# Value products of two heads side by side in the column halves of the array, gathered by six in two attentions

## The chip, the cores and the metric

The kernel runs on one core of one Trainium2 chip. The metric is the device time of one execution in microseconds (us). Engines: TensorE (PE: matmuls; PEld: its weight loads), VectorE (DVE), ScalarE (ACT), GpSimd (POOL) and SyncE (SP), which issues the DMAs.

## The reference, cut to what matters

The program is three transformer layers one after another over 512 tokens, width 1024. There are four attentions, and only they are touched here:

```python
# first layer, 16 meta keys beside the 512:
attn = softmax(s1) - lam * softmax(s2); y_a = attn @ v     # "diff": 4 heads, values 128 wide
y_b = softmax(s_window, sink) @ v                           # "win": 8 heads, values 64 wide
# second layer: dense causal, 8 heads, keys 96 wide, values 64 wide ("mla")
y_mla = softmax(causal(q @ k.T)) @ v
# third layer ("nsa"), 16 heads, values 64 wide, three gated branches per head:
y = g0 * (p_cmp @ vc) + g1 * (p_slc @ vs) + g2 * (p_win @ vw)
```

With 512 tokens the selected blocks and the 512 window both come to plain causal attention, so "nsa" has two causal branches (b = 0, 1) and one over 31 compressed keys. Everything else is projections and MLPs, each product made from three f16 matmuls (lines 845 to 847).

## The kernel before, in words

**Slots, tiles, units, chunks.** An attention is a run of slots. A slot is one head (and in "nsa" one branch of one head). Two heads (half 0 and half 1) make one output tile of 128 rows, 64 rows a head: half 0 gives rows 0 to 63, half 1 rows 64 to 127. "diff" is different: its two slots are the two softmaxes of one head whose values are 128 wide. So a tile is 2 slots, in "nsa" 4. Runs: "mix" is 8 slots of diff, then 8 of win; "mla" has 8 slots; "nsa" has 32 (8 tiles).

Each slot is worked twice. First the natural pass: queries on partitions, three or four *chunks* (`nat_scores`, line 947, with a mask product at 953 or 955) in two PSUM banks in turn; VectorE takes the row maximum (`nat_max`, line 1738), ScalarE the exponentials with their sums (`nat_exp`, line 1256). From these come a log-sum per row, which is split into f16 pieces (`split_lse`), turned by TensorE (`turn_lse`, line 1019) and written as extra rows of the queries (`lse_to_rows`, line 1804). Then the key pass: keys on partitions, three or four *units* (`key_scores`, lines 978 and 986) in three PSUM banks; ScalarE writes exp, already normalised, to one of four f32 tiles `tmp` (`key_exp`, line 1273), and TensorE multiplies with the values into the PSUM bank of the tile (`unit_values`, line 1006; an *extra* unit with all small keys of a tile at line 1003, its scores at 972). The causal units of a slot have one product of 512 columns, one of 384 and one of 128, and one of 256. The f32 value products are two instructions each. The 64 value columns of a head stand beside 64 columns of zeros (`vzm`, `vz`, zeroed by two memsets), so that each product writes all 128 rows and adds nothing to the other head's.

**Order.** The order is written out by hand and the same on all engines. The natural pass runs `ahead` slots before the key pass (4 in mix and nsa, 3 in mla). So a run begins with `ahead` slots of chunks alone (the prologue), then has slots with chunks and units, and its last `ahead` slots have units alone. Within a slot TensorE goes by steps:

```python
key_scores(t, i); [turn_lse]; nat_scores(nxt, i); unit_values(t.u + i - 2)
```

ScalarE per step does the exponential of this step's unit, then the one of the last step's chunk. The waits that pace this are: a unit's scores wait for the exponential three units back, a chunk's for the one two chunks back, an exponential of a unit for the value product four units back (its tile in `tmp`), a value product for its exponential.

Of the kernel before, what the change touches and what calls it, by code (L numbers as in the profile page):

```python
# [19 lines left out]

# [14 lines left out]
P = 128  # L35
# [181 lines left out]
class Slot:  # L217
# [3 lines left out]
    def __init__(self, kind, j, half, b, c, u, lse, y):  # L221
# [6 lines left out]
        self.c, self.u, self.lse, self.y = c, u, lse, y  # L228
        self.n_units = len(self.keys) + self.extra


class Run:
# [3 lines left out]
    def __init__(self, kinds, ahead, c, u, lse, y):  # L236
        self.slots, self.pre, self.ahead = [], [], ahead
        self.branches = kinds[0].branches
# [5 lines left out]
        for k in kinds:  # L244
            for j in range(k.tiles):
                for half in range(2):
                    for b in range(k.branches):
                        s = Slot(k, j, half, b, c, u, lse, y)
                        self.slots.append(s)
# [23 lines left out]
    def joined(self, s):  # L273
        t = self.at(s + 3)
# [23 lines left out]
UNITS = {s.u + i: (s, i) for s in ALL_SLOTS for i in range(s.n_units)}  # L298
# [153 lines left out]
def build_program(nc, x_in, stream, consts, params, aux, out):  # L452
    ctx = ExitStack()
    with ctx:
# [72 lines left out]
        def pair(at, shape):  # L527
# [34 lines left out]
            "p (a b c) -> p a b c", a=NQ, b=4)  # L562
        cqs, at = pair(at, [6, T])
# [29 lines left out]
        def values(t, kb):  # L593
# [3 lines left out]
            a = t.half * HD  # L597
            if t.kind.name == "win":
                return vw[:, kb, a:a + P]
            if t.kind.name == "mla":  # L600
                return vzm[:, kb, t.j, a:a + P]
            at = t.j // 4 * 3 * HD + a
            return vz[:, kb, t.b, at:at + P]

        def extra_values(t):
# [3 lines left out]
            return vmw if t.kind.name == "win" else vcz[:, 2 * (t.j // 4) + t.j % 2, :]  # L609

# [200 lines left out]
        def _(pe):  # L811
# [146 lines left out]
            def key_scores(t, i):  # L958

                u = t.u + i  # L960
# [28 lines left out]
            def unit_values(u):  # L989

                t, i = UNITS[u]
                new = t.first and i == 0
                end = t.last and i == t.n_units - 1
                if new and t.y >= 2:
# [4 lines left out]
                pe.wait_ge(key_exped, u + 1)  # L999
                p = tmp[:, u % 4, :]  # L1000
                o = y_bank(t.y)
                if i == len(t.keys):
                    mm = pe.matmul(o, extra_values(t), p, start=False, stop=end)  # L1003
                else:
                    for n_, (kb, c0, q0, n) in enumerate(t.keys[i]):
                        mm = pe.matmul(o[:, q0:q0 + n], values(t, kb), p[:, c0:c0 + n], start=new and n_ == 0,  # L1006
                                       stop=end and n_ == len(t.keys[i]) - 1)
                mm.then_inc(unit_av, 1)

            def turn_lse(t):  # L1010

                pe.wait_ge(lse_split, t.lse + 1)
                if t.kind.name in ("diff", "win"):
                    e = (t.tile + (8 if t.kind.name == "win" else 0)) // 2 - 1
# [12 lines left out]
            def attention(run):  # L1027

                for kind, n, c in run.pre:
                    extra_scores(kind, n, c)  # L1030
                for s in range(-run.ahead, run.n):
                    t, nxt = run.at(s), run.at(s + run.ahead)
                    if t is not None and (t.b == 0):
                        pe.wait_ge(lse_rows, t.lse + 1)
                    e = run.ended(s - 2)
                    if e is not None and e.kind.name == "diff":
                        sum_squares(e.j)
                    for i in range(run.steps(s)):
                        if t is not None and i < t.n_units:
                            key_scores(t, i)  # L1040
# [4 lines left out]
                        if t is not None and i < t.n_units and t.u + i >= run.u0 + 2:  # L1045
# [1334 lines left out]
```

## Time and profile before

| | |
|---|---|
| median of 3 runs | 2185.51 us (2184.99 to 2186.41) |
| the profiled execution, its own time | 2186.2 us |
| its span | 2184.4 us |
| TensorE busy | 2071.3 us (95%) |
| VectorE, ScalarE busy | 1195.7 us (55%), 817.0 us (37%) |
| mean granted TensorE clock | 0.964 of full |

The span is the time from the first to the last instruction in the trace; the execution's own time lies 1.8 us around it. A record of a matmul holds its latency too: in a stream the distance between starts, not the record's length, is what one costs. The clock is given as a share of 2.4 GHz.

### The profile page before, as it was taken

The numbers are of one execution on the slowest core, as the hardware profiler recorded it, in microseconds if no ns is written. First come the engines' busy times: TensorE is split into PE (matmuls) and PEld (weight loads), VectorE is DVE, ScalarE is ACT, GpSimd is POOL, SyncE is SP. The second block draws the span as 40 slices with busy tenths as digits, with TensorE's granted clock in tenths as the row PEclk, the third lists the DMA queues.
The fourth block names the chain that finished last, engine by engine and source line by source line (L and its number), as shares of the span: only waits on it lengthen the run. The fifth ranks groups of instructions, "written<-read, shape, count | busy, mean of one in ns | idle before, by whom it ended". The sixth has DMA issues, their size and how long they took to land. (4 is left out here: it accounts for less than half of the span.)

```text
span 2184.4 us, 27324 instructions
## 1 busy us (share of the span) xinstructions
PE 2071.3 (95%) x10625; PEld 1008.3 (46%) x10625; DVE 1195.7 (55%) x2186; ACT 817.0 (37%) x1481; POOL 38.5 (2%) x40
## 2 busy tenths in 40 slices
PE   7989999999999989989899999899799998999996
PEld 3444544444444434445344444355456653444442
DVE  5956744546554348665576522367555545855222
ACT  3437732323232222445343222234167742422220
POOL 2000000000000002000000000000000000000000
PEclk9979999999999999999899999898889998999998
DMA  6300133324333313212143333235000021433311
GB/s 196 107 1 1 59 87 106 97 77 126 106 97 116 97 49 116 87 39 87 39 132 100 107 105 97 77 109 174 11 1 1 20 87 29 145 101 102 109 46 39
DMA packets 52184, 179.18 MB, mean 82 GB/s; under 512 B 5984, under 2 KB 9696, under 8 KB 51680
## 3 DMA queue, kind: packets, MB, share of 16 engines
q1 hardware_dynamic: 52064, 177.51, 27.2%
q8 instruction: 84, 1.38, 0.3%
q14 instruction: 36, 0.29, 0.0%
HBM read 174.34 MB, written 2.10 MB: 81 GB/s over the span
## 5 line engine op out<-in xcount | busy, mean ns | idle before, releaser
L1540 DVE SCALAR_TENSOR_TENSOR w_lo<-w_raw,w_hi 128x1024 f16<-128x1024 f32 x317 | 385.4, 1219 | 181.4 <-ACT w_hi L1202 161.1
L1202 ACT ACTIVATE w_hi<-w_raw 128x1024 f16<-128x1024 f32 x317 | 331.0, 1049 | 277.4 <-PE pS L847 271.3
L845 PE MATMUL pS<-arena,w_hi 128*128 128x512 f16 x924 | 350.2, 379 | 5.0 <-DVE w_lo L1540 3.1
L845 PE MATMUL pS<-xx,w_hi 128*128 128x512 f16 x928 | 352.6, 380 | 1.4 <-DVE xx L1555 1.4
L846 PE MATMUL pS<-xx,w_hi 128*128 128x512 f16 x928 | 352.5, 380 | 0.0
L847 PE MATMUL pS<-xx,w_lo 128*128 128x512 f16 x928 | 352.4, 380 | 0.0
L846 PE MATMUL pS<-arena,w_hi 128*128 128x512 f16 x924 | 350.2, 379 | 0.0
L847 PE MATMUL pS<-arena,w_lo 128*128 128x512 f16 x924 | 350.2, 379 | 0.0
L1211 ACT ACTIVATE arena<-src 128x512 f16<-128x512 f32 x106 | 66.7, 629 | 325.1 <-DVE src L2113 168.2
L1595 DVE TENSOR_TENSOR tmp<-pS,rs 128x512 f32<-128x512 f32 x98 | 67.5, 689 | 140.2 <-PE pS L847 140.2
L1006 PE MATMUL pO<-tmp,arena 128*128 128x512 f32 (+3 forms) x384 | 144.1, 475 | 0.0
L845 PEld LDWEIGHTS pS<-arena,w_hi 128*128 128x128 f16 x924 | 90.5, 98 | 115.4 <-DVE w_lo L1540 3.6
L847 PEld LDWEIGHTS pS<-xx,w_lo 128*128 128x128 f16 x928 | 90.9, 98 | 110.2 <-issue 1.1
L847 PEld LDWEIGHTS pS<-arena,w_lo 128*128 128x128 f16 x924 | 90.4, 98 | 109.1
L846 PEld LDWEIGHTS pS<-arena,w_hi 128*128 128x128 f16 x924 | 90.4, 98 | 108.7 <-issue 0.3
L845 PEld LDWEIGHTS pS<-xx,w_hi 128*128 128x128 f16 x928 | 91.0, 98 | 107.4 <-DVE xx L1555 2.2
L846 PEld LDWEIGHTS pS<-xx,w_hi 128*128 128x128 f16 x928 | 90.9, 98 | 105.4 <-issue 1.5
L1273 ACT ACTIVATE tmp<-pS 128x256 f32<-128x256 f32 (+2 forms) x184 | 99.4, 541 | 71.8 <-PE pS L986 40.6
L889 PE MATMUL pS<-xx,w_hi 128*128 128x512 f16 x192 | 77.8, 405 | 30.0 <-DVE xx L1555 15.8
L978 PE MATMUL pS<-arena 128*128 128x512 f16 (+3 forms) x480 | 103.9, 314 | 1.3 <-DVE arena L1804 1.3
L2091 DVE TENSOR_SCALAR xx<-pS 128x512 f32<-128x512 f32 x24 | 16.6, 692 | 144.3 <-PE pS L847 144.3
L1738 DVE TENSOR_REDUCE st_max<-pS 128x1 f32<-128x512 f32 (+2 forms) x112 | 55.9, 517 | 64.4 <-PE pS L955 46.6
(319 smaller groups left out, 2822.2 us busy)
## 6 DMA issues: line engine op xcount, KB each, us to landing
w_raw<-in_w SPq DMA_DIRECT2D x317, 512.0 KB, 3.6
X<-in_x SPq DMA_DIRECT2D x1, 2112.0 KB, 8.2
arena<-in_c SPq DMA_DIRECT2D x2, 1024.0 KB, 5.5
out_t<-X SPq DMA_DIRECT2D x8, 256.0 KB, 2.0
arena<-in_h SPq DMA_DIRECT2D x4, 256.0 KB, 14.7
arena<-in_h SPq DMA_DIRECT2D x2, 512.0 KB, 9.1
arena<-in_c SPq DMA_DIRECT2D x2, 256.0 KB, 2.8
arena<-arena SPq DMA_DIRECT2D x4, 128.0 KB, 2.5
```

The source lines that it names most:

```text
L845: pe.matmul(ps, wh, ah, start=f, stop=False)
L846: pe.matmul(ps, wh, al, start=False, stop=False)
L847: mm = pe.matmul(ps, wl, ah, start=False, stop=l)
L889: pe.matmul(ps, wh, xa[0][:, k, 0:T], start=k == 0, stop=False)
L978: pe.matmul(ps[:, c0:c0 + n], k[:, ks_], q[:, qs], start=x == 0, stop=False)
L1006: mm = pe.matmul(o[:, q0:q0 + n], values(t, kb), p[:, c0:c0 + n], start=new and n_ == 0, stop=end and n_ == len(t.keys[i]) - 1)
L1202: act.activation(w_hi[:, u % WR, :], w_raw[:, u % RAW, :], ACT.Copy, scale=WS).then_inc(hi_split, 1)
L1211: act.activation(dst, a, ACT.Identity, scale=scale).then_inc(rhs_hi, 1)
L1273: act.activation(tmp[:, u % 4, 0:a.shape[1]], a, ACT.Exp).then_inc(key_exped, 1)
L1540: dve.scalar_tensor_tensor(out=w_lo[:, u % WR, :], in0=w_raw[:, u % RAW, :], scalar=WS, in1=w_hi[:, u % WR, :], op0=ALU.mult, op1=ALU.subt ...
L1595: dve.tensor_tensor(dst, ps, r[:, 0:T], ALU.mult).then_inc(evicted, 1)
L1738: ins = dve.tensor_reduce(stat(st_max, t)[:, x:x + 1], nat_bank(c)[:, c0:c0 + n], AX.X, ALU.max, negate=True)
```

## The change

For win, mla and nsa (`paired`), the zeros beside the values go: a value product has 64 stationary columns and writes only the 64 rows of its own head, `o[rows, ...]`. The units of the two heads of a tile alternate (`number`), so that products for the lower and the upper column half follow one another. In win two units are multiplied together; in mla and nsa six, that is, all units of two heads and one branch. The six wait for the last of their exponentials and are issued when its unit lies two or more units back. For this the exponentials get eight tiles in mla and nsa: the four of `tmp` and four more in space that is free then (`p_mla`, `cbias`). The extra unit stays one product of 128 columns. Both heads' log-sums must be there before a tile's first unit, so the natural pass runs further ahead: 5 slots in mix, 4 in mla, 6 in nsa; the log-sum steps move one slot (nsa: two) earlier with it. `turn_lse` and `sum_squares`, which share a PSUM bank, get a wait for the copy out of it. Two memsets of VectorE go. The diff slots keep their products.

```diff
-        self.c, self.u, self.lse, self.y = c, u, lse, y
+        self.c, self.lse, self.y = c, lse, y
         self.n_units = len(self.keys) + self.extra
+        self.paired = kind.name != "diff"
+        self.u, self.u_end = [], u
...
+        self.values, self.todo = [], defaultdict(list)
...
-                        u += s.n_units
                     lse += 1
+                u = self.number(self.slots[-2 * k.branches:], u)
...
+    def number(self, group, u):
+
+        if group[0].paired:
+            b = len(group) // 2
+            order = [(group[x + h * b], i) for x in range(b) for i in range(len(group[0].keys)) for h in range(2)]
+            order += [(group[-1], len(group[0].keys))] * group[-1].extra
+            n = 2 if group[0].kind.name == "win" else 6
+            self.values += [list(range(u + x, u + x + n)) for x in range(0, 6 * b, n)]
+            self.values += [[u + 6 * b]] * group[-1].extra
+        else:
+            order = [(t, i) for t in group for i in range(t.n_units)]
+            self.values += [[u + x] for x in range(len(order))]
+        for n, (t, i) in enumerate(order):
+            t.u.append(u + n)
+            self.todo[min(n * len(group) // (len(order) - group[0].paired * group[-1].extra), len(group) - 1) + group[0].s].append((t, i))
+        for t in group:
+            t.u_end = u + len(order)
+        return u + len(order)
...
-        return self.at(s + 2 + (not odd)) if s % 2 == odd else None
+        return self.at(s + 4 + (not odd)) if s % 2 == odd else None
 
     def summed(self, s):
-        return self.head(s, 2, 0)
+        return self.head(s, 3, 0)
 
     def turned(self, s):
-        return self.head(s, 1, 1)
+        return self.head(s, 2, 1)
 
     def joined(self, s):
-        t = self.at(s + 3)
+        t = self.at(s + 4)
...
-        return max(a.n_units if a else 0, len(b.nat) if b else 0, 3)
+        return max(len(self.todo[s]) if a else 0, len(b.nat) if b else 0, 3)
+
+    def unit(self, s, i):
+
+        return self.todo[s][i] if 0 <= s < self.n and i < len(self.todo[s]) else None
...
-    for name, kinds, ahead in (("mix", ("diff", "win"), 4), ("mla", ("mla",), 3), ("nsa", ("nsa",), 4)):
+    for name, kinds, ahead in (("mix", ("diff", "win"), 5), ("mla", ("mla",), 4), ("nsa", ("nsa",), 6)):
...
+        p_mla, _ = view(at, [4, T])
...
-            a = t.half * HD
+            a = 2 * t.half * HD
             if t.kind.name == "win":
-                return vw[:, kb, a:a + P]
+                return vw[:, kb, a:a + HD]
             if t.kind.name == "mla":
-                return vzm[:, kb, t.j, a:a + P]
+                return vzm[:, kb, t.j, a:a + HD]
             at = t.j // 4 * 3 * HD + a
-            return vz[:, kb, t.b, at:at + P]
+            return vz[:, kb, t.b, at:at + HD]
...
+        def p_more(t):
+
+            return {"mla": [p_mla[:, n, :] for n in range(4)], "nsa": [cbias[:, n, :] for n in range(4)]}.get(t.kind.name, [])
+
+        def p_tile(t, u):
+
+            more = p_more(t)
+            n = (u - RUNS[t.kind.name].u0) % 8 if more else u % 4
+            return tmp[:, n, :] if n < 4 else more[n - 4]
...
-            def unit_values(u):
-
-                t, i = UNITS[u]
-                new = t.first and i == 0
-                end = t.last and i == t.n_units - 1
-                if new and t.y >= 2:
+            def unit_values(us):
+
+                t, i = UNITS[us[0]]
+                if t.first and i == 0 and t.y >= 2:
                     if t.y < 6:
                         pe.wait_ge(y_scaled, t.y - 1)
                     else:
                         pe.wait_ge(rhs_ready, Y_RHS[t.y - 2] + 1)
-                pe.wait_ge(key_exped, u + 1)
-                p = tmp[:, u % 4, :]
+                pe.wait_ge(key_exped, us[-1] + 1)
                 o = y_bank(t.y)
                 if i == len(t.keys):
-                    mm = pe.matmul(o, extra_values(t), p, start=False, stop=end)
-                else:
+                    pe.matmul(o, extra_values(t), p_tile(t, us[0]), start=False, stop=True,
+                              skip_group_check=t.paired).then_inc(unit_av, 1)
+                    return
+                for x in range(0, len(us), 2):
+                    i = UNITS[us[x]][1]
                     for n_, (kb, c0, q0, n) in enumerate(t.keys[i]):
-                        mm = pe.matmul(o[:, q0:q0 + n], values(t, kb), p[:, c0:c0 + n], start=new and n_ == 0,
-                                       stop=end and n_ == len(t.keys[i]) - 1)
-                mm.then_inc(unit_av, 1)
+                        for u in us[x:x + 2]:
+                            t = UNITS[u][0]
+                            rows = head_rows(t.half) if t.paired else slice(0, P)
+                            new = t.b == 0 and i == 0 and n_ == 0 and (t.paired or t.first)
+                            mm = pe.matmul(o[rows, q0:q0 + n], values(t, kb), p_tile(t, u)[:, c0:c0 + n], start=new, stop=False,
+                                           skip_group_check=t.paired)
+                            if n_ == len(t.keys[i]) - 1:
+                                mm.then_inc(unit_av, 1)
 
             def turn_lse(t):
 
                 pe.wait_ge(lse_split, t.lse + 1)
+                if t.lse:
+                    pe.wait_ge(lse_rows, t.lse)
...
+                left = list(run.values)
                 for s in range(-run.ahead, run.n):
                     t, nxt = run.at(s), run.at(s + run.ahead)
-                    if t is not None and (t.b == 0):
+                    if t is not None and t.first:
+                        pe.wait_ge(lse_rows, t.lse + 1 + t.paired)
+                    elif t is not None and not t.paired:
                         pe.wait_ge(lse_rows, t.lse + 1)
                     e = run.ended(s - 2)
                     if e is not None and e.kind.name == "diff":
+                        if run.turned(s - 1):
+                            pe.wait_ge(lse_rows, run.turned(s - 1).lse + 1)
                         sum_squares(e.j)
                     for i in range(run.steps(s)):
-                        if t is not None and i < t.n_units:
-                            key_scores(t, i)
+                        now = run.unit(s, i)
+                        if now:
+                            key_scores(*now)
                         if i == 1 and run.turned(s):
                             turn_lse(run.turned(s))
                         if nxt is not None and i < len(nxt.nat):
                             nat_scores(nxt, i)
-                        if t is not None and i < t.n_units and t.u + i >= run.u0 + 2:
-                            unit_values(t.u + i - 2)
-                unit_values(run.u1 - 2)
-                unit_values(run.u1 - 1)
+                        while now and left[0][-1] <= now[0].u[now[1]] - 2:
+                            unit_values(left.pop(0))
+                for us in left:
+                    unit_values(us)
...
-                if u >= 4:
-                    act.wait_ge(unit_av, u - 3)
-                act.activation(tmp[:, u % 4, 0:a.shape[1]], a, ACT.Exp).then_inc(key_exped, 1)
+                n = len(p_more(t)) + 4
+                if u >= RUNS["mix" if t.kind.name in ("diff", "win") else t.kind.name].u0 + n:
+                    act.wait_ge(unit_av, u - n + 1)
+                act.activation(p_tile(t, u)[:, 0:a.shape[1]], a, ACT.Exp).then_inc(key_exped, 1)
...
-            link(dve.memset(vzm[:, :, :, HD:2 * HD], 0.0))
...
-            link(dve.memset(vz, 0.0))
```

## Rows read from the trace of the kernel before

**Rows 1.** Page, busy time by engine over the span

```profile
PE 2071.3 (95%) x10625; PEld 1008.3 (46%) x10625; DVE 1195.7 (55%) x2186; ACT 817.0 (37%) x1481; POOL 38.5 (2%) x40
```

**Rows 2.** Stretches: span, length, PE, PEld, DVE, ACT, POOL busy, clock, DMA share, GB/s

```profile
1618.40:1640.60 22.20, 22.15 (x144) 13.85 (x143) 12.52 (x40) 16.10 (x50) 0.00 (x0) 1.00 0.00 1
1455.00:1475.00 20.00, 20.00 (x215) 15.76 (x214) 17.42 (x29) 7.82 (x11) 0.00 (x0) 0.79 0.89 248
```

**Rows 3.** Chain that ended last, nsa: start, us, the three value products of a slot

```profile
1601.28 0.91 PE pO L1006 x2
...
1603.17 0.92 PE pO L1006 x4
...
1605.41 0.49 PE pO L1006 x2
```

**Rows 4.** Timeline, nsa: start us, us; scores of four extra units, once per tile

```profile
1617.53 1.03 PE L972 MATMUL pS<-arena 128*128 128x512 f16 x4
1639.69 1.03 PE L972 MATMUL pS<-arena 128*128 128x512 f16 x4
1751.59 1.03 PE L972 MATMUL pS<-arena 128*128 128x512 f16 x4
1768.09 1.03 PE L972 MATMUL pS<-arena 128*128 128x512 f16 x4
```

**Rows 5.** Timeline, mla: first units of two successive slots, with chunks and without

```profile
975.05 0.81 PE L978 MATMUL pS<-arena 128*128 128x512 f16 x3
981.31 0.81 PE L978 MATMUL pS<-arena 128*128 128x512 f16 x3
1000.07 0.81 PE L978 MATMUL pS<-arena 128*128 128x512 f16 x3
1004.47 0.81 PE L978 MATMUL pS<-arena 128*128 128x512 f16 x3
```

**Rows 6.** Timeline, win: first unit of three successive tiles

```profile
242.03 0.38 PE L978 MATMUL pS<-arena 128*128 128x256 f16 x2
256.26 0.38 PE L978 MATMUL pS<-arena 128*128 128x256 f16 x2
266.12 0.38 PE L978 MATMUL pS<-arena 128*128 128x256 f16 x2
```

**Rows 7.** Timeline: matmuls of 128 and of 16 output rows in turn

```profile
85.58 0.38 PE L846 MATMUL pS<-xx,w_hi 128*128 128x512 f16 x1
85.80 0.38 PE L847 MATMUL pS<-xx,w_lo 128*128 128x512 f16 x1
86.11 0.38 PE L863 MATMUL pT<-w_hi,xx 128*16 128x512 f16 x1
```

**Rows 8.** Timeline: eight f32 weight loads in a row with matmuls of one column

```profile
37.73 0.97 PEld L905 LDWEIGHTS pO<-ones,acc 128*128 128x128 f32 x8
```

**Rows 9.** Timeline, ScalarE in nsa: a unit and the chunk right behind it

```profile
1599.51 0.60 ACT L1273 ACTIVATE tmp<-pS 128x512 f32<-128x512 f32 x1 [0.48 <-PE pS L986]
1600.01 0.66 ACT L1256 ACTIVATE pS<-pS,st_max 128x512 f32<-128x512 f32 x1
```

**Rows 10.** Waits of ScalarE in nsa, 1589 to 1772: us, times, longest

```profile
ACT tmp L1273 <- PE pS L986: 32.1, 65, 0.9
ACT tmp L1273 <- DVE src L1767: 12.7, 8, 2.1
```

**Rows 11.** Timeline, prologues: slot's first chunk, nsa (ScalarE) and mix (TensorE)

```profile
1585.23 0.66 ACT L1256 ACTIVATE pT<-pT,st_max 128x512 f32<-128x512 f32 x1 [1.04 <-DVE st_max L1738]
1589.34 0.66 ACT L1256 ACTIVATE pS<-pS,st_max 128x512 f32<-128x512 f32 x1 [1.01 <-DVE st_max L1738]
...
145.41 0.75 PE L947 MATMUL pS<-arena 128*128 128x512 f16 x2 [0.66 <-ACT pS L1256]
...
150.61 0.61 PE L947 MATMUL pS<-arena 128*128 128x512 f16 x1 [0.38 <-ACT pS L1256]
```

**Rows 12.** Groups by line: the larger memset

```profile
L2130 DVE MEMSET arena<- 128x3072 f32 x1 | 2.6, 2618 | 0.6 <-issue 0.6
```

More of the change, by code:

```diff
@@ L21 @@
+from collections import defaultdict
 from contextlib import ExitStack
@@ L248, in __init__ @@
                         s = Slot(k, j, half, b, c, u, lse, y)
+                        s.s = len(self.slots)
                         self.slots.append(s)
                         c += len(k.nat)
-                        u += s.n_units
                     lse += 1
+                u = self.number(self.slots[-2 * k.branches:], u)
                 y += 1
@@ L297 @@
 CHUNKS = {s.c + i: (s, i) for s in ALL_SLOTS for i in range(len(s.nat))}
-UNITS = {s.u + i: (s, i) for s in ALL_SLOTS for i in range(s.n_units)}
+UNITS = {s.u[i]: (s, i) for s in ALL_SLOTS for i in range(s.n_units)}
 Y_RHS = {s.y: PL.r[s.kind.rhs] + s.j for s in ALL_SLOTS}
@@ L958, in key_scores @@
             def key_scores(t, i):
-                u = t.u + i
+                u = t.u[i]
                 if u == RUNS["mla"].u0:
@@ L998, in unit_values @@
                         pe.wait_ge(rhs_ready, Y_RHS[t.y - 2] + 1)
-                pe.wait_ge(key_exped, u + 1)
-                p = tmp[:, u % 4, :]
+                pe.wait_ge(key_exped, us[-1] + 1)
                 o = y_bank(t.y)
                 if i == len(t.keys):
-                    mm = pe.matmul(o, extra_values(t), p, start=False, stop=end)
-                else:
-                    for n_, (kb, c0, q0, n) in enumerate(t.keys[i]):
-                        mm = pe.matmul(o[:, q0:q0 + n], values(t, kb), p[:, c0:c0 + n], start=new and n_ == 0,
-                                       stop=end and n_ == len(t.keys[i]) - 1)
-                mm.then_inc(unit_av, 1)
+                    pe.matmul(o, extra_values(t), p_tile(t, us[0]), start=False, stop=True,
[3 more added lines that the diff above has]
+                    i = UNITS[us[x]][1]
+                    for n_, (kb, c0, q0, n) in enumerate(t.keys[i]):
+                        for u in us[x:x + 2]:
[6 more added lines that the diff above has]
+                                mm.then_inc(unit_av, 1)
             def turn_lse(t):
                 pe.wait_ge(lse_split, t.lse + 1)
+                if t.lse:
+                    pe.wait_ge(lse_rows, t.lse)
                 if t.kind.name in ("diff", "win"):
-                    e = (t.tile + (8 if t.kind.name == "win" else 0)) // 2 - 1
+                    e = (t.tile - 1 + (8 if t.kind.name == "win" else 0)) // 2 - 1
                     if e > 0:
@@ L1259, in key_exp @@
             def key_exp(t, i):
-                u = t.u + i
+                u = t.u[i]
                 if t.kind.name == "nsa" and i == len(t.keys):
@@ L1333, in attention @@
                     for i in range(run.steps(s)):
-                        if t is not None and i < t.n_units:
-                            key_exp(t, i)
+                        if run.unit(s, i):
+                            key_exp(*run.unit(s, i))
                         if pending is not None:
@@ L1761, in cmp_bias @@
             def cmp_bias(t):
[L1763 removed]
+                u = t.u[len(t.keys)]
                 dve.wait_ge(key_scored, u + 1)
@@ L1857, in attention @@
                             nat_max(nxt, i)
-                        if t is not None and t.kind.name == "nsa" and t.extra and i == len(t.keys):
-                            cmp_bias(t)
+                        now = run.unit(s, i)
+                        if now and now[0].kind.name == "nsa" and now[1] == len(now[0].keys):
+                            cmp_bias(now[0])
                         if i == 0 and run.joined(s):
```

5 lines of the change are left out of this document (2 added, 3 removed).

## The prediction

> **What bounds the kernel now.** I began with the page's busy times: TensorE is busy for 2071.3 of 2184.4 us [rows 1]. The chain of waits says the same inside nsa, the longest attention: it runs through value products, which take 0.91, 0.92 and 0.49 us for the three units of a slot [rows 3], 2.32 us a slot. Then the stretches: of one nsa tile of four slots (22.20 us) TensorE works 22.15, ScalarE 16.10, VectorE 12.52 [rows 2]. So nsa is bound by TensorE, and ScalarE has only about a quarter of the time free. Last the timeline, for the lengths of a tile: 22.16 us while chunks of the natural pass run beside it, 16.50 in the last slots, which have none [rows 4]. In mla a slot is 6.26 with chunks, 4.40 without [rows 5]; in win a tile is 14.23 with, 9.86 without [rows 6].
>
> From these, nsa's key pass is 7 tiles with chunks and 1 without, 7 x 22.16 + 16.50 = 171.6 us; mla's is 5 x 6.26 + 3 x 4.40 = 44.5. A chunk costs TensorE (22.16 - 16.50) / 12 = 0.47 us, a unit's scores (16.50 - 4 x 2.32 - 0.91 - 0.9 for the extra unit's two parts, - 0.4 for two turns) / 12 = about 0.4.
>
> **Step 1, the products.** A group of six holds 2 x 2.32 = 4.64 us of products, in 16 instructions. If an instruction for the lower column half streams while its neighbour for the upper half does, the group takes half, 2.32. The two instructions of one product use the same half, so only the second of one runs beside the first of the next; at the edges one 512 and one 256 instruction stand alone, (0.46 + 0.24) / 2 = 0.35. And the array changes between 128 and 64 columns twice a group. The nearest row is the change to 16 output rows: starts 0.31 apart instead of 0.22 [rows 7], so 0.09 a change, 0.18 a group. Together 2.85: **1.8 us less a group**, if the streams overlap. No row shows an overlap. Its bounds are 2.32 (all of it and no edges) and 4.64 + 0.18 (none). I take the overlap: the instructions are adjacent and share neither output rows nor columns. The Trainium skill measured it on narrow f16 tiles (TensorE: Matmul & The Clock Gate, section "Measured speedup vs the span model"): three column tiles ran 2.38 times as fast as one after another. No run here shows that yet, and no number of mine uses it.
>
> Weight loads must be hidden too. Eight f32 loads of 128 columns in a row took 0.97 us [rows 8], 0.12 each; those of 64 columns lie between half of that and that. Two per instruction pair of 0.46 us fit, even at 0.21.
>
> **Step 2, what ScalarE makes of the groups (nsa with chunks).** TensorE alone would need 22.16 - 2 x 1.8 = 18.6 a tile. But during a group it feeds ScalarE nothing. ScalarE's need is 16.10 of busy time less the tail of a record that the next instruction would overlap (0.60 recorded, 0.50 to the next start [rows 9]), about 73 / 8 = 9 times a tile [rows 10]: 15.2. How much can it have in hand when a group starts? The chunk issued just before waited for the chunk two back, so there is one unit's exponential (0.50) and one chunk (0.66). The next chunk stands in its queue behind the next unit's exponential, whose scores are behind the group on TensorE. So it stands still for 0.47 (last chunk) + 2.85 + 0.4 (next scores) - 1.16 = 2.6 us a group. Twice that, and part of the wait for the extra unit's bias on VectorE, up to 12.7 / 8 = 1.6 now [rows 10], of which I keep 0.6: 15.2 + 5.2 + 0.6 = **21.0 us a tile**, bounds 20.0 and 22.0. Eight tiles of exponentials do not help here: what is missing is scores, three banks of them. So only 1.2 of the 3.6 us reach the end.
>
> **Step 3, running further ahead.** A prologue slot is chunks alone, a round trip TensorE, VectorE, ScalarE: 4.11 us in nsa, 5.20 in mix [rows 11]; for mla, the same chunks as nsa, I take 4.1. nsa gets two more, mla and mix one. What they did before beside units is then gone there: two nsa slots, one mla, one win.
>
> **The sum.**
> nsa: 6.5 tiles x 21.0 + 1.5 x (16.50 - 3.6) + 2 x 4.11 = 136.5 + 19.4 + 8.2 = 164.1, against 171.6: -7.5.
> mla: TensorE's three passes leave ScalarE more room. A group with chunks is 12.52 - 1.8 = 10.7 against ScalarE's (15.2 - 1.1) / 2 + 2.6 = 9.7, so TensorE rules. 2 x 10.7 + 2 x (8.80 - 1.8) + 4.1 = 39.5, against 44.5: -5.0.
> mix: +5.2 for the prologue; one win slot without chunks, -(14.23 - 9.86) / 2 = -2.2; win's products, some 4.4 us a tile, become 2.2 + 0.9 of edges (three pairs) + 6 x 0.09 = 3.6, -0.8 x 4, of which I count -2.0 because two tiles run beside chunks. +1.0.
> Memsets: 2.6 us [rows 12] and a smaller one a third as large on VectorE; TensorE is busy all of the 20.00 us around the larger [rows 2], so 0; 3.5 us if that cover were gone. The new waits in `turn_lse` and `sum_squares` are for a copy a slot old: 0; were it late, all of TensorE stands behind it, some 0.5 us (one copy) in each of 32 places. No DMA or queue changes.
> Sum -11.5. From the profiled execution, 2186.2, that is 2174.7; the median of the runs lies 0.7 lower: **2174 us**. With step 2's bounds, 2167 to 2181.
>
> **The rivals.**
> *ScalarE keeps up.* If it has more in hand at a group's start (chunks ahead of the unit in its queue), a tile is TensorE's 18.6: 6.5 x 2.4 = 15.6 less, 2158. For it: 6.1 us free a tile [rows 2]. Against: the queue order above.
> *No overlap: slower.* If f32 products in two column halves run one after the other, a group is 4.64 + 0.18, and ScalarE stands still 2.6 + 2.0 = 4.6 each. A tile is 15.2 + 9.2 + 0.6 = 25.0, nsa 6.5 x 25.0 + 1.5 x 16.9 + 8.2 = 196, +24.5; mla 2 x 12.7 + 2 x 9.0 + 4.1 = 47.5, +3.0; mix 5.2 - 2.2 + 24 x 0.09 = +5.2. 2218. It decides once a group exceeds about 3.6 us: each 0.1 costs some 2 us. For it: every one of the present narrow matmuls (16 rows) still takes a full stream [rows 7], though all of those are in one column position. This is also the case where the change does not do what it says.
> *Overlap, but the weight loads show.* 16 loads a group at 0.06 to 0.12 are 1.0 to 1.9 us, in 20 groups and four win tiles: +24 to +46 on 2174, held below the last rival; 2200. Against: now the loads run under the streams. The skill (same page, "What overlaps and what doesn't") says a load overlaps running matmuls only when its row group differs; all loads here use all rows. By that rule this rival would be the case. The trace does not agree for full-width products: a tile has 13.85 us of loads in 22.15 of matmuls and no more time than the streams [rows 2].
>
> **How the numbers follow.** My forecast 0.46; ScalarE keeps up 0.20; no overlap 0.18; loads show 0.08; the rest, near no change, 0.08. A measurement of this kernel tells some 0.2% (4.4 us) from no change. Faster: 0.44 + 0.20 + a little of the rest, 0.66; slower: 0.18 + 0.08, 0.26; within: 0.08. The range takes in the forecast, the fast rival and the loads: 2156 to 2203; the forecast's own is 2167 to 2181.
>
> **What would show it.** Groups of 16 instructions on line 1006's successor taking 2.8 to 2.9 us from first to last start; over 4.6 is the second rival, 3.8 or more the third. An nsa tile of 21 us with ScalarE idle 2.6 before a unit's exponential after each group; 18.6 is the first rival. Six nsa prologue slots of about 4.1. An mla group with chunks of 10.7. What makes me wrong most easily is step 2: a slot of ScalarE's queue more or less in hand moves 13 groups by 0.5 us each.

## The result, and the profile after

The changed kernel takes **2189.62 us** (median of 20 runs, 2187.59 to 2191.02), the kernel before 2185.52 in the same comparison (2183.92 to 2190.24): ratio 1.0014, 95% interval 1.0008 to 1.0021. The forecast was 2174. TensorE does save its time and the execution gets no shorter, as two lines of the page say beside [rows 1]:

```profile
span 2186.3 us, 27318 instructions
PE 2034.4 (93%) x10625; PEld 964.9 (44%) x10625; DVE 1191.9 (55%) x2184; ACT 814.2 (37%) x1481; POOL 38.5 (2%) x40
```

TensorE is busy 36.9 us less than before, and the span is 1.9 us longer. Where that went is read stage by stage, from the first and last starts of the lines that score chunks and units. A prologue runs from the first chunk's matmul to the first unit's, a key pass from there to the first matmul behind the attention (us):

| | mix: prologue, key pass, sum | mla | nsa | nsa tile with chunks |
|---|---|---|---|---|
| before | 24.5, 120.4, 144.9 | 14.8, 45.9, 60.7 | 19.5, 176.8, 196.3 | 22.16 |
| changed | 30.3, 113.8, 144.1 | 19.1, 43.9, 63.0 | 28.9, 167.8, 196.7 | 21.82 |
| difference | +5.8, -6.6, **-0.8** | +4.3, -2.0, **+2.3** | +9.4, -9.0, **+0.4** | |
| forecast | **+1.0** | **-5.0** | **-7.5** | 21.0 |

The three differences make the span's 1.9 us. The forecast's -11.5 misses it by 13.4, of which mla and nsa hold 15.2.

**The overlap is there, and whole.** The timeline at the start of a group, columns: start, duration, engine, line, operation, operands:

```profile
1618.65 0.20 PEld L1049 LDWEIGHTS pO<-tmp,arena 128*64 128x64 f32 x4
1618.65 0.65 PE L1049 MATMUL pO<-tmp,arena 128*64 128x512 f32 x2
```

Two products for different column halves start together (x2 in one record from 1618.65), and their weights and those of the next two are loaded in the first 0.2 us. The chain of waits through a tile, below, has groups of 16 instructions at 2.30 us, where the two slots' products took 4.64 [rows 3].

**What an nsa tile is made of now.** The window of one tile (busy us and instructions of TensorE, its loads, VectorE, ScalarE, GpSimd), and the stretch that holds the large memset in the kernel before [rows 2]:

```profile
1640.50:1662.30 21.80, 18.80 (x145) 10.28 (x144) 12.43 (x40) 15.77 (x51) 0.00 (x0) 1.00 0.00 1
1455.00:1475.00 20.00, 20.00 (x199) 14.93 (x198) 17.81 (x30) 10.47 (x16) 0.00 (x0) 0.84 0.98 274
```

Before, TensorE worked 22.15 of 22.20 us; now it stands still for 3.0 of 21.80, and no engine is busy throughout. The memset's stretch is full of TensorE's work as it was. The waits of all engines from 1607 to 1770 us (total, times, longest):

```profile
PEld pT L986 <- ACT pT L1308: 20.6, 27, 1.1
ACT tmp L1326 <- PE pS L1025: 14.7, 11, 2.2
ACT arena L1326 <- PE pS L1025: 14.6, 12, 2.2
PE pT L986 <- ACT pT L1308: 14.1, 20, 0.9
```

ScalarE waits for scores (29.3 us), and TensorE for the bank of a chunk that ScalarE has not released (14.1). A view of waits can't say which of them matters. The chain of waits can, here over one tile:

```profile
1662.36 2.30 PE pO L1049 x16
1664.66 0.43 PE pS L1017 x2
...
1665.32 0.22 PE pS L986 x2
1665.54 0.07 PE pS L994
1665.61 0.02 issue
1665.63 0.42 DVE st_max L1791
1666.05 0.08 DVE lse L1832
...
1667.78 0.21 DVE lse_cols L1844
1667.98 0.57 DVE st_max L1791
...
1669.16 0.20 ACT pT L1308
1669.36 0.05 issue
1669.41 0.39 PE pT L986 x2
1669.80 0.06 PE pT L994
1669.86 0.86 PE pS L1011 x4
...
1671.69 2.30 PE pO L1049 x16
```

The rows show three engines in a ring, that is, a loop of waits that has to be gone round before the next tile can be as far. After its group TensorE scores a chunk; VectorE takes the maximum, then its 10 small log-sum operations (`split_lse`, 1666.05 to 1667.98, 1.93 us), and only then the next chunk's maximum; ScalarE exponentiates that chunk; TensorE gets its bank. The same happens once more in the tile, from 1677.34 to 1679.27, and there another VectorE operation (line 1608, 0.56 us) stands before the maximum as well. Before the change the chain went through no VectorE operation at all between 1607 and 1700 us.

### The profile page after: what moved, and what is told of

It reads as the page before. It is cut to its first block and busy times, and to the rows that moved or that the text cites. A ratio compares the mean times of both kernels' runs of the same rounds, so it can differ in the third digit from the quotient of the medians.

```text
span 2186.3 us, 27318 instructions
## 1 busy us (share of the span) xinstructions
PE 2034.4 (93%) x10625; PEld 964.9 (44%) x10625; DVE 1191.9 (55%) x2184; ACT 814.2 (37%) x1481; POOL 38.5 (2%) x40
## 5 line engine op out<-in xcount | busy, mean ns | idle before, releaser
L1608 DVE SCALAR_TENSOR_TENSOR arena<-src,arena 128x512 f16<-128x512 f32 x106 | 72.8, 687 | 26.6 <-ACT arena L1263 26.4
L1791 DVE TENSOR_REDUCE st_max<-pS 128x1 f32<-128x512 f32 (+2 forms) x112 | 55.8, 516 | 57.5 <-PE pS L994 45.7
L1326 ACT ACTIVATE tmp<-pS 128x512 f32<-128x512 f32 (+2 forms) x124 | 67.3, 550 | 46.4 <-PE pS L1025 18.1
## 6 DMA issues: line engine op xcount, KB each, us to landing
arena<-in_h SPq DMA_DIRECT2D x4, 256.0 KB, 14.8
```

The source lines that it names most:

```text
L1326: act.activation(p_tile(t, u)[:, 0:a.shape[1]], a, ACT.Exp).then_inc(key_exped, 1)
L1608: dve.scalar_tensor_tensor(out=dst, in0=a, scalar=scale, in1=h, op0=ALU.mult, op1=ALU.subtract).then_inc(rhs_ready, 1)
L1791: ins = dve.tensor_reduce(stat(st_max, t)[:, x:x + 1], nat_bank(c)[:, c0:c0 + n], AX.X, ALU.max, negate=True)
```

## The experiments

Each is compared with the kernel before on the same chip, with a 95% interval of the ratio. "The tile" is an nsa tile beside chunks.

### One part alone, and the overlap taken away

**Only the running ahead** (e1): the kernel before with the later starts of the changed one.

```
-("mix", ("diff", "win"), 4), ("mla", ("mla",), 3), ("nsa", ("nsa",), 4)
+("mix", ("diff", "win"), 5), ("mla", ("mla",), 4), ("nsa", ("nsa",), 6)
-        return self.at(s + 2 + (not odd)) if s % 2 == odd else None
+        return self.at(s + 4 + (not odd)) if s % 2 == odd else None
...
```

> The kernel before with the natural pass 5, 4 and 6 slots ahead (and the log-sum steps and waits moved as in the change), products as before. Theory: the longer prologues are a cost of their own: +5.8 (mix), +4.3 (mla), +9.3 us (nsa) of prologue, and what leaves the key pass is 0.47 us a chunk in nsa, 1.86 a slot in mla, 2.2 a slot in mix: -2.2, -1.9, -3.8. Sum +11 to +12 us against before, 2197. Rival (a prologue slot is worth what it takes away): within 2 us of before.

2196.79 us, 1.0045 (1.0028 to 1.0061), 10.5 slower than the 2186.31 of its comparison. Sums: mix 148.9, mla 63.0, nsa 201.3, together 11.3 more than before; the tile 22.16. So the change carries a debt of some 11 us. Against this kernel, the new products give back 4.8 in mix, nothing in mla and 4.6 in nsa.

**No two neighbours in different halves** (e2): the same groups, but first all products of one head, then all of the other.

```
+parts = ... if len(us) < 6 else [[u] for h in range(2) for u in us[h::2]]
-                        for u in us[x:x + 2]:
+                        for u in part:
```

> The changed kernel, but within a group of six all products of one head come before all of the other, so that two in a row use the same column half. Theory (half the time of a group comes from products of the two halves running side by side, and what a group takes ScalarE stands idle): a group takes 4.6 instead of 2.3 us, and the whole of it reaches the end in all 20 groups: +40 to +46 us against the changed kernel, about 2232. Rival (another chain bounds the attentions now, and the products are no longer on it): under +15.

2220.29 us, 1.0152 (1.0135 to 1.0168), 30.7 above the changed kernel and not 40 to 46. The sign and the mechanism are the theory's; its 4.6 us a group is not. One group in the timeline, up to the first score behind it:

```profile
1678.04 1.07 PE L1050 MATMUL pO<-tmp,arena 128*64 128x512 f32 x2
1678.94 0.92 PE L1050 MATMUL pO<-arena 128*64 128x384 f32 x3
1679.60 0.64 PE L1050 MATMUL pO<-tmp,arena 128*64 128x512 f32 x1
1679.70 0.70 PE L1050 MATMUL pO<-arena 128*64 128x128 f32 x3
...
1681.90 0.50 PE L1017 MATMUL pS<-arena 128*128 128x384 f16 x2
```

The group takes 3.86 us. The 512 columns at 1679.60 are the other head's first: they start when three of the first head's eight instructions have yet to start, so where the two heads meet, some of the overlap is left. From 2.30 to 3.86 is 1.56 us a group: 31.2 in 20 groups, against 30.7 measured, and 3.1 in the two groups of a tile, which takes 24.92 instead of 21.82. All that was added to a group reached the end. Only the order of the instructions differs, so the overlap comes from instructions of different halves standing close together. That the rival of no overlap had 25.0 for this tile is luck: its group was 4.82.

### Which loop holds the nsa tile

**Pairs everywhere** (e3), eight tiles for exponentials as before:

```
-            n = 2 if group[0].kind.name == "win" else 6
+            n = 2
```

> The changed kernel with products gathered by two everywhere, eight tiles kept. Theory (ScalarE starves for as long as a group lasts): no stretch without scores is over about 1 us, an nsa tile goes from 21.8 to about 19.5, mla gives 4 us more: 2170, with 0.18 us of column changes a pair counted. Rival (the round trip of the chunks TensorE, VectorE, ScalarE bounds a tile whatever the grouping): 2187 or more.

2177.74 us, 0.9963 (0.9949 to 0.9977): faster than both kernels. mla's sum falls from 63.0 to 57.5, nsa's from 196.7 to 192.2, and the tile only to 21.35. The theory gave 19.6 us and 11.9 came: 5.5 in mla, more than it said, but 0.47 a tile in nsa, where it said 2.3. Long groups cost something, and in nsa they are not all of it. TensorE works 19.41 us in a tile of 21.34, against 18.80 with six: pairs keep most of the overlap.

**Groups behind the next unit's scores** (e4), so that ScalarE has one unit more in hand when a group starts:

```
                             key_scores(*now)
+                        if now and len(left[0]) == 6 and left[0][-1] <= now[0].u[now[1]] - 3:
+                            unit_values(left.pop(0))
```

> The changed kernel, but a group of six is issued one unit later, between the next unit's scores and its chunk, so that ScalarE has one more exponential and the chunk behind it in hand while the group runs. Theory: ScalarE's idle of 2.2 us at a group falls by about 1.2 us (0.5 + 0.66 of work in hand), in 13 groups of nsa and 2 of mla: -15 to -18 us, 2172. Rival (chunks' round trip): within 4 us of the changed kernel, 2189.

2184.38 us, 0.9985 (0.9975 to 0.9994). The tile stays at 21.81. ScalarE does have more in hand: its waits for scores from 1607 to 1716 us fall from 19.2 to 12.1. The forecast had made the tile out of ScalarE's standstill behind a group, and with the standstill shorter the tile is the same. The median is still 5.2 us below the changed kernel's, a little outside the rival's 4; part of it lies where no chunks run beside a group (the last nsa tile takes 13.93 instead of 14.95).

**Shorter exponentials** (e11):

```
+                if t.kind.name == "nsa" and t.tile > 3:
+                    a = a[:, 0:256]
                 act.activation(p_tile(t, u)[:, 0:a.shape[1]], a, ACT.Exp)
```

> The changed kernel, but from the fifth head on the third attention's unit exponentials take only the first 256 of their columns (the rest of each probability tile keeps what was there, so the output is not the reference's): 0.39 us instead of 0.60. Nothing else changes. Theory: after the overlap, each step of the tile is a trip TensorE, ScalarE, TensorE, in which a shorter exponential shows in full: about 8 of 0.20 us a tile, so that the tile falls from 21.8 to about 20.3 in the last four heads, and the median by 5, to 2184. Rival: TensorE's own work and VectorE's column set the tile, and ScalarE with some 6 us idle in it has room: less than 0.3 us a tile, 2188 to 2190.

2187.29 us, 1.0008 (0.9998 to 1.0017). Its window of one tile:

```profile
1648.02:1669.84 21.82, 18.74 (x145) 10.30 (x144) 12.38 (x41) 14.20 (x50) 0.00 (x0) 1.00 0.00 1
```

1.6 us less of ScalarE's work in a tile, and 21.82 still. So the trip through the unit's exponential is not what sets the tile here. Whether it comes just behind, this run can't say.

**The log-sum block in parts** (e5, e6, e7). Its 10 operations are cut in two or three and put behind different chunks' maxima, in the changed kernel, in pairs, and in the kernel before.

```
-                        if i == 2 and run.summed(s):
-                            split_lse(run.summed(s))
+                        if run.branches == 2:
+                            if i in (1, 2) and run.summed(s):
+                                split_lse(run.summed(s), (i - 1,))
+                            if i == 0 and run.summed(s - 1):
+                                split_lse(run.summed(s - 1), (2,))
+                        elif i in (1, 2) and run.summed(s):
+                            split_lse(run.summed(s), (0,) if i == 1 else (1, 2))
```

> The changed kernel with the log-sum pieces (11 small VectorE instructions, 2.1 us in one block between two chunk maxima) cut into two or three parts that follow three different chunk maxima. Theory B (the block holds back the next chunk's maximum, so ScalarE's chunk, so the bank, so TensorE): an nsa tile falls from 21.8 to 20 or less, -12 us or more against the changed kernel, 2178. Theory A (ScalarE starves while a group of six runs, nothing else): within 3 us of 2189.

> The same spreading with products by twos. Theory B: with both waits gone TensorE is the bound again (19.5 us busy in a tile by twos): tile 21.35 to about 19.7, -12 us against products by twos alone, 2166. Theory A: as products by twos alone, 2178.

> The kernel before with the same spreading. Both theories: TensorE is the bound there, the block is hidden: within 1.5 us of before. If it gains more, the block was already a cost before the change.

Measured: 2206.93 (1.0097, 1.0080 to 1.0114), 2182.91 (0.9988, 0.9978 to 0.9998) and 2194.04 (1.0038, 1.0023 to 1.0052). All three are slower than the same kernel with the block whole, and e5 was missed by some 15 us at the least. Its waits from 1607 to 1770 us say why the edit was a bad test:

```profile
PEld pT L1065 <- DVE lse_cols L1855: 20.6, 13, 3.1
PE pT L1065 <- DVE lse_cols L1855: 17.7, 13, 2.9
```

TensorE, which turns the pieces a slot later, now waits up to 2.9 us for the last part. Spreading exchanged one wait for another; it tells nothing of the block's own price.

**The block left out** (e8):

```
+                if nb == 3 and t.tile > 1:
+                    dve.tensor_scalar(lse_pieces(t, 0), ..., ALU.min, ALU.mult).then_inc(lse_split, 1)
+                    return
```

> The changed kernel with the log-sum pieces of nsa left out from the third head on (one VectorE instruction in place of 11; the rows that normalise are then not the reference's). Theory B: the tile falls at least as far as with the pieces spread, to 19.5 to 20: 2176 or less. Theory A: 2189.

2187.27 us, 1.0006 (0.9997 to 1.0016), the tile 21.37. By itself that speaks against the block. But the chain of waits is now another one:

```profile
1640.12 2.31 PE pO L1049 x16
1642.42 0.43 PE pS L1017 x2
...
1643.11 0.03 ACT arena L1326
1643.14 0.46 issue
1643.61 0.35 ACT pT L1308
1643.96 0.11 issue
1644.07 0.56 ACT pT L1308 x3
1644.63 0.05 issue
1644.68 0.60 PE pT L986 x2
```

TensorE finishes its group and scores a unit; ScalarE does that unit's exponential, and only behind it the chunk's; TensorE waits for the chunk's bank. A second ring, 0.45 us shorter than the first.

**The chunk's exponentials ahead of the unit's** (e10), which opens the second ring:

```
+                        if pending is not None:
+                            nat_exp(pending)
+                            pending = None
                         if run.unit(s, i):
                             key_exp(*run.unit(s, i))
-                        if pending is not None: ...
```

> The changed kernel, with the chunk's exponentials ahead of the unit's in ScalarE's order at every step. Theory: TensorE waits for the bank that the chunk's exponential frees (14.1 us of waits in 163 us of the third attention), and that exponential stands behind a unit's of 0.60 us that waits for newer scores; put first, the third attention's tile falls from 21.8 to 20.8 to 21.3, about 2183. Rival: the chunk's exponential waits for VectorE's maximum and then holds the unit's, whose scores bank TensorE needs in its turn: the tile stays at 21.8 or grows to 22.5, 2189 to 2197.

2190.27 us, 1.0022 (1.0012 to 1.0031), the tile 21.82: the rival's figure. Its reason is half of it: the chunk's exponential does wait for a maximum, but for one that stands behind the block. The chain still has the block's two stretches of VectorE at the same places.

**Both at once** (e13), the edits of e8 and e10:

> The changed kernel with both edits that alone gave the third attention little or nothing: VectorE's log-sum block cut to one operation from the third head on (so the output is not the reference's), and the chunk's exponentials ahead of the unit's. Theory: the tile of six has two loops of nearly one length, one through VectorE's block (21.82 us, which an exponential elsewhere can't shorten) and one through ScalarE's order (21.37 us, which shows once the block is gone); with both cut the tile falls to TensorE's 18.8 plus some 1 us, 19.5 to 20.3, and the median to 2174 to 2179. Rival: a third thing holds it, and the tile stays at 21.3 or more, 2186 to 2188.

2173.04 us, 0.9945 (0.9928 to 0.9961). Its window of one tile:

```profile
1622.92:1642.41 19.49, 18.22 (x145) 10.38 (x143) 9.62 (x23) 15.66 (x51) 0.00 (x0) 1.00 0.01 1
```

The four tiles in groups of six, side by side:

| | unit's exponential first | chunk's first |
|---|---|---|
| VectorE's block whole | 21.82 | 21.82 |
| block left out | 21.37 | 19.49 |

One edit gives 0, the other 0.45, both 2.33. That is what two rings of nearly one length do, and it settles the cause for the nsa tile beside chunks. The last tile, which has no chunks, is 14.95 in all four; in pairs (e3) it is 13.37.

**Pairs, chunk's exponentials first** (e12), the edits of e3 and e10:

> Groups of two units everywhere, eight tiles for exponentials, and the chunk's exponentials ahead of the unit's. If the theory of the run before holds, 2171 to 2175, faster than both kernels and than the pairs alone (2177.7). Rival: no better than 2177.

2171.68 us, 0.9933 (0.9916 to 0.9949), the tile 20.20. The order alone helps in pairs, by 1.15 us a tile. The chain's shares by line in e3, from 1607 to 1720 us, say why:

```profile
by line: PE pO L1049 24.9%; ACT pT L1308 18.6%; PE pS L1017 14.7%; PE pT L986 14.2%; issue 10.7%; PE pS L1011 4.3%; PE pO L1039 4.0%; PE pS L1025 2.7%; PE pT L994 2.1%; PE pS L986 1.9%; ACT arena L1326 1.0%; ACT tmp L1326 0.7%; PE pS L994 0
```

In pairs it passes through ScalarE's exponentials of chunks (18.6%), and VectorE's maxima are not among its main lines: there the ring that the order opens is the longer one. With it open (e12) the block is back in the chain, with 9.8% for the maxima and 9.9% for the block's copies and subtractions (lines 1844 and 1850), so that 20.20 is the block's ring in pairs.

**The kernel before with that order** (e15), the edit of e10 without the change:

> The kernel before, with only the chunk's exponentials ahead of the unit's. Theory: before the change TensorE sets the third attention's tile alone (it waits for ScalarE nowhere in it), so that this order gives nothing without the overlap: tile 22.1 to 22.2, median within 1.5 us of before. Rival: the order gives its some 1 us a tile in any kernel: 2176 to 2180.

2186.05 us, 1.0003 (0.9993 to 1.0012), the tile 21.94 instead of 22.16. The order is worth 0.22 us a tile where TensorE is the bound, a little more than expected, and the median doesn't show it.

### What holds mla

**No look-ahead at weight units in mla** (e9, and e16 in the kernel before), the same edit on VectorE:

```
-                    if s >= run.n - WR:
+                    if s >= run.n - WR and run.slots[0].kind.name != "mla":
                         split_hi(look_tau, most=1)
```

> The changed kernel, but neither ScalarE nor VectorE looks ahead for weight units during the second attention; the eight units are split after it. Theory: in the second attention a group of six gains nothing because one weight split per slot (ScalarE 1.06 us, VectorE 1.22 us) stands between two exponentials, which the forecast left out. Then its key pass falls from 43.9 to 38 to 40 us, and up to 8 us come back as TensorE's waits for weights behind it, so that the median lands between 2186 and 2194. Rival: the key pass is bound by the six exponentials themselves in either case: it stays within 1 us of 43.9.

> The kernel before, with no look-ahead at weight units in the second attention. Theory: there TensorE is the bound and the splits lie beside it: key pass 45.9 as before, median within 2 us of before or later by the waits for weights behind the attention. Rival: leaving them out gains some 5 us with or without the change.

e9: 2183.35 us, 0.999 (0.9981 to 1.0); its mla key pass is 39.4 instead of 43.9, and the median falls by 6.3, more than expected; the 1.8 beyond the key pass were not followed up. e16: 2185.30 us, 1.0003 (0.9993 to 1.0012), key pass 45.9 as before. ScalarE's timeline of the changed kernel in one mla group shows the work that the forecast left out:

```profile
987.49 0.19 ACT L1308 ACTIVATION_READ_ACCUMULATOR pS<-pS,st_max 128x1 f32 x1
989.78 0.60 ACT L1326 ACTIVATE tmp<-pS 128x512 f32<-128x512 f32 x1 [2.10 <-PE pS L1025]
...
991.65 1.07 ACT L1254 ACTIVATE w_hi<-w_raw 128x1024 f16<-128x1024 f32 x1
992.59 0.61 ACT L1326 ACTIVATE tmp<-pS 128x512 f32<-128x512 f32 x1
```

A split of 1.07 us in every mla slot stands before a unit's exponential that is already late. TensorE's groups in the changed kernel, and then in e9:

```profile
986.50 1.94 PE L1049 MATMUL pO<-tmp,xx 128*64 128x512 f32 x12
...
998.42 1.08 PE L1049 MATMUL pO<-arena,xx 128*64 128x512 f32 x4
...
1006.88 1.94 PE L1049 MATMUL pO<-arena,xx 128*64 128x512 f32 x12
```

```profile
985.49 1.94 PE L1049 MATMUL pO<-tmp,xx 128*64 128x512 f32 x12
...
996.19 1.08 PE L1049 MATMUL pO<-arena,xx 128*64 128x512 f32 x4
...
1003.17 1.94 PE L1049 MATMUL pO<-arena,xx 128*64 128x512 f32 x12
```

From one group's start to the next with chunks it is 11.92 us with the splits and 10.70 without; the next 8.46 and 6.98. The forecast had 10.7 and 7.0.

The splits are not all of it. Pairs (e3) keep the splits and take the same key pass to 38.4, further than e9 does in groups of six. In pairs leaving them out gives 1.6 more (e14, below), in six it gives 4.5. The cost is that of a split and a long group together.

### The parts put together

**Pairs, chunk's exponentials first, no look-ahead in mla** (e14), the edits of e3, e10 and e9:

> Groups of two everywhere, the chunk's exponentials first, and no look-ahead at weight units in the second attention. Theory: the second attention's key pass loses 2 to 4 us of its 38.4, as it did in groups of six, and the median is 2167 to 2170. Rival: in pairs ScalarE has the time for the splits; the key pass stays at 38 and the weights come late behind it, 2172 to 2178.

2170.69 us, 0.9936 (0.9919 to 0.9952). mla's key pass is 36.7 instead of 38.4; the median is 1.0 below e12's, less than these runs can tell apart.

**The block on GpSimd** (e17 in six, e18 in pairs), whole, added to the order and the edit of e9. In nsa VectorE's 10 operations become 11 of GpSimd's (one of VectorE's does two steps that are two operations there):

```
+            for h in range(16):
+                t = RUNS["nsa"].slots[2 * h]
+                pool.wait_ge(lse_ln, t.lse + 1)
+                pool.wait_ge(lse_split, t.lse)
+                pool.wait_ge(lse_turned, t.lse)
+                step(pool.tensor_tensor(a, m, lse_l[:, 0:3, :], ALU.subtract))
...
```

> Groups of six, the chunk's exponentials first, no look-ahead at weight units in the second attention, and in the third the log-sum block moved whole from VectorE to GpSimd, which idles there (12 operations on 128 by 12, the same results). Theory: with the block off VectorE and the order changed, the tile of six is what it was with the block left out, 19.5 to 20.0 us, and the median the changed kernel's 2189.6, less 14.9 (third attention's key pass 153.0 instead of 167.9) and less 6.3 (no look-ahead): about 2168, 2166 to 2171. Rival: GpSimd takes so long for the block (one of its powers takes about 1 us in the profile, with two there) that TensorE's turn, one slot later, waits for it: tile 21 us or more, 2178 or more.

> The same with groups of two everywhere. Theory: pairs are left with the same loop through ScalarE that gave 20.20 a tile, and with less work on VectorE: 19.6 to 20.2, median 2166 to 2171. Rival: as there, GpSimd is late, 2175 or more.

e17: **2167.49 us**, 0.9919 (0.9903 to 0.9936), the tile 19.49. e18: **2161.76 us**, 0.9892 (0.9876 to 0.9909), the tile 18.63, better than its expectation, which took 20.20 for ScalarE's ring. First and last GpSimd operation of one head in e17, then a tile's window in e18:

```profile
1647.81 0.21 POOL L861 TENSOR_TENSOR lse<-st_max,lse_l 128x12 f32<-128x12 f32 x1 [6.76 <-ACT lse_e L1386]
...
1650.71 0.24 POOL L874 CAST lse_cols<-lse 128x12 f16<-128x12 f32 x1
```

```profile
1633.83:1652.46 18.63, 18.63 (x144) 10.11 (x143) 9.42 (x20) 15.54 (x52) 4.92 (x22) 1.00 0.00 1
```

The block takes GpSimd 3.14 us instead of VectorE's 1.93, and TensorE waits for it once in e17, 2.4 us from 1600 to 1760. In e18 TensorE is busy for the whole tile again. e17's tile equals that of e13, which left the block out: the block's cost was its place in VectorE's queue.

## Why the prediction was wrong, step by step

**Step 1 held, and was too careful.** A group takes 2.30 us, not 2.85. The chain shows no price of edges or of changes of the array, and no loads: the third rival is out. The Trainium skill's rule that the third rival rested on (TensorE: Matmul & The Clock Gate, section "What overlaps and what doesn't": a load overlaps running matmuls only where its row group differs) is not borne out by this trace, in which four loads on all rows end 0.20 us into two streams that began with them. The same page's section "Measured speedup vs the span model" gives 2.38 for three column tiles 32 wide (it names no type, so the prediction's "f16" is not on it); the trace agrees that column tiles overlap, and has 4.64 / 2.30 = 2.0 for two here. e2 shows that it hangs on the order: where few instructions of different halves stand close together, a group is 3.86.

**Step 2 failed in its path, and by 0.8 us a tile in its size.** It took the tile as ScalarE's work and standstill, 15.2 + 5.2 + 0.6 = 21.0. The standstill is real (2.10 us before a unit's exponential behind a group, in the rows of mla above). But e11 took 1.6 us of ScalarE's work away and e4 gave ScalarE more in hand, and the tile did not move. What sets 21.82 is a ring over three queues in order, in which VectorE's block of 1.93 us stands between two maxima. Hard behind it, at 21.37, lies one through ScalarE's order (e8, e13): the chunk's exponential behind the unit's, whose scores are behind the group, which is the order that the step described. So the step had the second ring, near its 21.0, and missed the first. The step looked at VectorE only as 12.52 of 22.20 us busy and so as free; its block is short, but it stands in front of the one maximum that is waited for. The first rival, TensorE's own 18.6 us a tile, is reached by e18 with 18.63, with the order of ScalarE that the rival named, in pairs, and with the block moved, which it did not name. That the two agree so closely is partly luck: 18.6 had 2.85 us in it for a group of six.

**The mla term failed: "TensorE rules" left out the weight splits.** It set 9.7 us of ScalarE against 10.7 of TensorE for a group. ScalarE also splits a weight unit of 1.07 us in each mla slot, two or more a group, and with them the group took 11.92. Without them it took 10.70 (e9), the number forecast, with some luck: with 2.30 for the products, the same sum gives 12.52 - 2.34 = 10.2. The term was to give -5.0 and gave +2.3. The key pass was to lose 9.1 us and lost 2.0. Of the 7.1 between, the splits are 4.5 (e9); most of the rest, 2.6, went only in e14, with pairs, the chunk's exponentials first and no splits (36.7, which is 9.2 below the 45.9 of before). In the kernel before the splits cost nothing (e16): TensorE was behind, and they lay beside it.

**Step 3 held, a little small.** Prologues cost 5.8, 4.3 and 9.4 us, against 5.2, 4.1 and 8.2; e1 has the whole debt at some 11, less than the 19.5 of prologues because the key passes gain from the chunks that left them. In mix the key pass won 6.6 us instead of the 4.2 that the term gave, so mix came to -0.8 and not +1.0.

**The sum.** mla is off by 7.3 us, nsa by 7.9 and mix by -1.8: 13.4 of the profiled execution, and the medians lie 2.2 further apart than the profiled spans. That is the way from 2174 to 2189.6. In nsa, the tiles beside chunks are 6.5 x 0.8 = 5.3 us of the miss and the prologues 1.1; the tile without chunks was put at 16.50 - 3.6 = 12.9 and takes 14.95, another 3.1 for the 1.5 of them, and what remains goes the other way. The memsets cost nothing, as forecast. The new waits were put at 0, and no row has TensorE held by one before a turn; what it waits for there is the block's last copy, 3.3 us from 1607 to 1770, a wait that was there before.

**What stays open.** Why six units in a group are worse than two even where both rings are open (19.49 against 18.63 a tile, with TensorE idle for 1.27 of it) no run isolates; ScalarE still stands up to 1.1 us for scores there (e13). The same holds for the last nsa tile, 14.95 in six and 13.37 in pairs. And why the second head's products in e2 start three instructions early, and not earlier or later, the runs do not say.

## What to carry to other kernels

When an engine that was the bound is made faster by a sixth, look at who stood just behind it, and not by busy shares: write down for each queue in order what stands between one item that the ring needs and the next. A small block in a half-idle engine, or a look-ahead that was free, can become the bound there. If one edit gives nothing and the chain of waits changes with it, try it together with the edit that opens the new chain before giving either up: here 0 and 0.45 alone made 2.33 together. And group no more work than the overlap needs: pairs had nearly the whole overlap and fed the other engines sooner.

## What the runs showed of the hardware

Two f32 matmuls of 128 rows by 64 columns, adjacent and in different column halves, start together and cost what one costs: 16 of them take 2.30 us. With all eight of one half before all eight of the other they take 3.86, not 4.64: the first of the second half starts while three of the first half have yet to start. Small operations in a chain cost more on GpSimd than on VectorE, but not by much: 11 on 128 by 12, nearly each waiting for the one before, took 3.14 us, and the same block in 10 on VectorE 1.93.
